# First activation chunk at another place in its 128-byte line, and the residual's transposes moved from the down projection into the up projection

## What is computed

```python
mix_out = jnp.einsum("bsd,de->bse", merged, w_out[layer])
x = x + rms_norm_2(mix_out, mix_norm_post[layer])
h = rms_norm_2(x, ffn_norm_pre[layer])
up = jnp.einsum("bsd,df->bsf", h, w_up[layer])
up = causal_dwconv(up, conv_f_w[layer], conv_f_b[layer])
gate, val = jnp.split(up, 2, axis=-1)
ffn_out = jnp.einsum("bsf,fd->bsd", jax.nn.gelu(gate) * val, w_down[layer])
x = x + rms_norm_2(ffn_out, ffn_norm_post[layer])
```

## Time and profile before

| | us |
|---|---|
| median of 3 runs (lowest, highest) | 1136.49 (1133.57, 1137.23) |
| the profiled execution, its own time | 1134.4 |
| its span, first to last instruction | 1132.6 |
| TensorE busy, of the span | 1109.1 |
| VectorE busy | 786.1 |
| ScalarE busy | 587.8 |
| GpSimd busy | 140.6 |

### The profile page before, as it was taken

How to read it: one execution, slowest core, us unless ns; L and a number is a source line. 1 busy time by engine, 2 the same in 40 slices (tenths; PEclk the granted TensorE clock), 3 DMA queues, 4 the chain that set the end, 5 groups by cost and what they waited for, 6 DMA issues and landing times.

```text
span 1132.6 us, 21593 instructions
## 1 busy us (share of the span) xinstructions
PE 1109.1 (98%) x9351; PEld 1068.6 (94%) x9351; DVE 786.1 (69%) x1134; ACT 587.8 (52%) x828; POOL 140.6 (12%) x109
## 2 busy tenths in 40 slices
PE   7999899999999999999999999999999989999998
PEld 6988799999999999999999997999988989999998
DVE  6567488784457566977644689786475889888752
ACT  4477655443336555544433566854366647666531
POOL 4200050001230005000122206201010000111000
PEclk9999999999999999999999999999999999999999
DMA  9943055566654444555555472666464545556551
GB/s 280 276 150 112 1 184 189 186 195 201 200 187 155 154 139 150 186 187 187 186 187 186 132 212 69 200 200 217 131 221 143 188 147 187 186 187 205 186 184 40
DMA packets 195938, 195.72 MB, mean 173 GB/s; under 512 B 9803, under 2 KB 193028, under 8 KB 195844
## 3 DMA queue, kind: packets, MB, share of 16 engines
q1 hardware_dynamic: 193680, 190.53, 52.9%
q10 hardware_dynamic: 2164, 3.82, 1.1%
HBM read 192.86 MB, written 1.47 MB: 172 GB/s over the span
## 4 chain that ended last, share of the span: by engine, by line
PE 94%; DVE 3%; ACT 2%; DMA 0%; issue 0%; DVEq 0%; SPq 0%; ACTq 0%
PE ps_gemm L1727 50%; PE ps_trans L1727 35%; PE ps_score L1804 2%; PE ps_out L1836 2%; PE ps_trans L1821 2%; DVE act_lo L1144 2%; DVE w_lo L1138 1%; PE ps_gemm L1908 1%; PE ps_score L2035 1%; DMA x_in<-in_x 0%; PE ps_out L2035 0%; PE ps_out L2039 0%; PE ps_score L2039 0%; DVE rs L1150 0%; PE ps_score L1770 0%; ACT prob L798 0%
## 5 line engine op out<-in xcount | busy, mean ns | idle before, releaser
L1138 DVE TENSOR_TENSOR w_lo<-raw,w_hi 128x2048 fp32r<-128x2048 f32 (+2 forms) x179 | 408.2, 2289 | 45.2 <-ACT w_hi L753 45.0
L753 ACT ACTIVATE w_hi<-raw 128x2048 fp32r<-128x2048 f32 (+2 forms) x179 | 332.3, 1863 | 175.2 <-DMA raw<-in_mlp_w 95.3
L1727 PE MATMUL ps_gemm<-act_hi,w_hi 128*128 128x256 f32 (+1 forms) x960 | 267.1, 286 | 4.7 <-ACT act_hi L1064 4.4
L1727 PE MATMUL ps_gemm<-act_hi,w_lo 128*128 128x256 f32 (+1 forms) x960 | 259.9, 282 | 0.0
L1727 PE MATMUL ps_gemm<-act_lo,w_hi 128*128 128x256 f32 (+1 forms) x960 | 254.8, 281 | 0.5 <-DVE act_lo L1144 0.4
L1727 PE MATMUL ps_trans<-act_hi,w_hi 128*128 128x256 f32 x688 | 193.1, 281 | 1.9 <-DVE w_lo L1138 1.9
L1727 PE MATMUL ps_trans<-act_hi,w_lo 128*128 128x256 f32 x688 | 193.0, 281 | 0.0
L1727 PE MATMUL ps_trans<-act_lo,w_hi 128*128 128x256 f32 x688 | 192.9, 280 | 0.0
L1727 PEld LDWEIGHTS ps_gemm<-act_hi,w_hi 128*128 128x128 f32 (+1 forms) x960 | 182.1, 192 | 10.2 <-issue 8.2
L1727 PEld LDWEIGHTS ps_gemm<-act_hi,w_lo 128*128 128x128 f32 (+1 forms) x960 | 178.6, 190 | 0.3
L1727 PEld LDWEIGHTS ps_gemm<-act_lo,w_hi 128*128 128x128 f32 (+1 forms) x960 | 173.7, 186 | 2.1 <-DVE act_lo L1144 0.9
(11 more groups left out here) (379 smaller groups left out, 2238.9 us busy)
## 6 DMA issues: line engine op xcount, KB each, us to landing
raw<-in_mlp_w SPq DMA_DIRECT2D x64, 1024.0 KB, 5.4
raw<-in_w_in SPq DMA_DIRECT2D x30, 1024.0 KB, 5.4
raw<-in_w_up SPq DMA_DIRECT2D x24, 1024.0 KB, 5.2
raw<-in_od_w_in SPq DMA_DIRECT2D x12, 1024.0 KB, 5.1
raw<-in_w_down SPq DMA_DIRECT2D x12, 1024.0 KB, 5.2
raw<-in_ev_w_in SPq DMA_DIRECT2D x9, 1024.0 KB, 8.1
raw<-in_w_proj_a SPq DMA_DIRECT2D x8, 640.0 KB, 4.3
raw<-in_ev_w_out SPq DMA_DIRECT2D x4, 1024.0 KB, 5.1
```

The lines of the kernel that those rows point to most:

```text
L753: act.activation(w_hi[:, slot, 0:k, 0:n], raw[:, slot, 0:k, 0:n], ACT.Copy).then_inc(hi_done, 1)
L1138: dve.tensor_tensor(w_lo[:, slot, 0:k, 0:n], raw[:, slot, 0:k, 0:n], w_hi[:, slot, 0:k, 0:n].bitcast(F32), ALU.subtract).then_inc(w_ready, 1)
L1727: ins = pe.matmul(dst, lhs, rhs, start=(first and opens and opening), stop=(last and closes and i + 1 == len(order)), skip_group_check=True)
```

## The change

Chunk 0 of `act_hi` gets a tensor of its own, 32 bytes past the place that it had; the other seven chunks start 1152 bytes past the old start, 128 more than before, and so keep their place in a 128-byte line. `act_lo` is laid out likewise. Scratch and arena start 256 bytes later. `act_hi` and `act_lo` become lists of chunks, so each use picks its chunk; `gemm` gets a small function for that. The 16 transposes of the residual stand behind slab 3 (the fourth) of `f_up`, no longer behind slab 2 of `f_dn`, with the same two waits. No instruction is added or dropped.

```diff
@@ -67,6 +67,8 @@
 PA = 8
 DN_STEP = 10
 RING = 5
+TURN_AT = 3
+FIRST_SHIFT = (32, 32)
 AHEAD = 3
 REL = 384

@@ -191,9 +193,17 @@
     ssq = place("ffn_sums", [P, TB, 4])
     rs_o = place("ffn_rs", [P, TB])
     fw = place("conv_f", [P, 4, 2 * NH2])
-    act_hi = place("act_hi", [P, NX, T], F32R)
-    act_lo = place("act_lo", [P, NX, T], F32R)
-    tmp0 = top[0]
+    acts = top[0]
+
+    def chunks(name, at, shift):
+
+        first = place(f"{name}_first", [P, T], F32R, at + shift)
+        rest = place(name, [P, NX - 1, T], F32R, at + T * 4 + P)
+        return [first[:, :]] + [rest[:, c, :] for c in range(NX - 1)]
+
+    act_hi = chunks("act_hi", acts, FIRST_SHIFT[0])
+    act_lo = chunks("act_lo", acts + NX * T * 4 + P, FIRST_SHIFT[1])
+    tmp0 = acts + 2 * (NX * T * 4 + P)
     arena = tmp0 + 8 * K
     assert arena + 70 * K <= 229344, arena + 70 * K

@@ -757,7 +767,7 @@
-                    act.activation(act_hi[:, c, :], x[:, c, :], ACT.Copy, scale=gain(n, c)).then_inc(xh, 1)
+                    act.activation(act_hi[c], x[:, c, :], ACT.Copy, scale=gain(n, c)).then_inc(xh, 1)
@@ -807,7 +817,7 @@
-                    dst = dob[:, o - 4, :] if pr["kind"] == "diff" else (mix_hi if p < 2 else act_hi)[:, o, :]
+                    dst = dob[:, o - 4, :] if pr["kind"] == "diff" else mix_hi[:, o, :] if p < 2 else act_hi[o]
@@ -1141,8 +1151,8 @@
-                dve.scalar_tensor_tensor(out=act_lo[:, c, :], in0=x[:, c, :], scalar=gain(n, c),
-                                         in1=act_hi[:, c, :].bitcast(F32), op0=ALU.mult, op1=ALU.subtract).then_inc(xl, 1)
+                dve.scalar_tensor_tensor(out=act_lo[c], in0=x[:, c, :], scalar=gain(n, c),
+                                         in1=act_hi[c].bitcast(F32), op0=ALU.mult, op1=ALU.subtract).then_inc(xl, 1)
@@ -1166,7 +1176,6 @@
-            hi, lo = (mix_hi, mix_lo) if p < 2 else (act_hi, act_lo)
@@ -1237,7 +1246,8 @@
-                    dve.tensor_tensor(lo[:, o, :], ps_o[:, seq % 2, 0:T], hi[:, o, :].bitcast(F32), ALU.subtract)\
+                    hi_o, lo_o = (mix_hi[:, o, :], mix_lo[:, o, :]) if p < 2 else (act_hi[o], act_lo[o])
+                    dve.tensor_tensor(lo_o, ps_o[:, seq % 2, 0:T], hi_o.bitcast(F32), ALU.subtract)\
@@ -1695,6 +1705,10 @@
+
+            def chunk(xx, c):
+                return xx[c] if isinstance(xx, list) else xx[:, c, :]
+
@@ -1715,13 +1729,13 @@
-                    lhs = xx[:, kc0 + k, half * P:(half + 1) * P]
+                    lhs = chunk(xx, kc0 + k)[:, half * P:(half + 1) * P]
-                    rhs = xx[:, kc0 + k, :]
+                    rhs = chunk(xx, kc0 + k)
@@ -2080,6 +2094,14 @@
         for j in range(24):
             gemm(s0 + j, g0 + j, act_hi, act_lo, before_chunk=x_in(6) if j == 0 else None, low_last=j == 0,
                  between=stat_at(6, 2) if j == 1 else None)
+            if j == TURN_AT:
+                pe.wait_ge(x_new, 4)
+                pe.wait_ge(sd_ok, 7)
+                for tb in range(TB):
+                    for c in range(NX):
+                        ins = pe.transpose((ps_s, ps_o)[tb][:, c // 4, c % 4 * P:(c % 4 + 1) * P],
+                                           x[:, c, tb * P:(tb + 1) * P], ident[:, :])
+                ins.then_inc(x_tok, 1)
         s0, g0 = st["f_dn"].s0, st["f_dn"].g0
         for j in range(12):
             def ready(pair, r=j % 3):
@@ -2087,14 +2109,6 @@
-            if j == 2:
-                pe.wait_ge(x_new, 4)
-                pe.wait_ge(sd_ok, 7)
-                for tb in range(TB):
-                    for c in range(NX):
-                        ins = pe.transpose((ps_s, ps_o)[tb][:, c // 4, c % 4 * P:(c % 4 + 1) * P],
-                                           x[:, c, tb * P:(tb + 1) * P], ident[:, :])
-                ins.then_inc(x_tok, 1)

```

More of the change, by code:

```diff
@@ L1063, in _ @@
             for c in (2 * gi, 2 * gi + 1):
-                act.activation(act_hi[:, c, :], x[:, c, :], ACT.Copy, scale=gain(6, c)).then_inc(xh, 1)
+                act.activation(act_hi[c], x[:, c, :], ACT.Copy, scale=gain(6, c)).then_inc(xh, 1)
             if gi == 2:
```

## The result

The changed kernel takes 1144.94 us in the median of six runs (1143.55 to 1147.63), the kernel before 1135.03 us beside it (six runs, 1128.69 to 1137.95): a ratio of 1.0107, 95% interval 1.0067 to 1.0147. It is slower, by about 1%. The profiled execution took 1143.55 us with a span of 1141.8 us, 9.2 us above the span of before.

What follows compares the result with a forecast made beforehand. TensorE's matmul spacing was taken as the bound. From 1134.4 us, 16.8 of fast slabs less 1.3 tipping delay and 0.6 borders, plus 0.1, gave 1119.4; allowing for the before median, 2.1 higher, 1119 to 1122, forecast 1121, range 1117 to 1146.

Steps and rivals of the forecast that it cites:

- What bounds the kernel: TensorE, busy 98% of the span: time is the number of L1727 matmuls times their start-to-start distance, at two paces.
- 0.215 us a slab: Claimed difference for 48 matmuls between the slow pace, 5.655 us, and the fast one, 5.440 us; nothing lies between.
- chunks 1 to 7 stay at 64: Activation layout: only chunk 0 changes its place in a 128-byte line; everything behind moves 256 bytes and keeps its place.
- The direct cost of the borders: Place changes around chunk 0 in 115 slabs, two borders each: 0 to 1.2 us, taken as 0.6.
- The Sum: Total for the whole kernel: borders tip 78 reachable slow slabs to fast, up to 16.8 us gained; fast case chance 0.50.
- a steady against an uneven beat: Reason given for the fast pace winning: the steady pace is absorbing, the slow one is an uneven beat of three.
- The borders tip the pace to slow: Rival: the fast pace doesn't survive chunk 0's border; up to 13.5 us lost, 1143 to 1150, middle 1147; chance 0.20.
- discount for what tips by chance: In the slow rival, an amount without its own figure taken off 1136.5 + 13.5, leaving 1143 to 1150.
- The transposes: 16 transposes moved from f_dn to f_up: about 1.75 us moves along, waits already met, net by itself -0.1 us.
- the two extras: At 946.3 in f_up: the 75 ns w_lo wait vanishes; such breaks led to fast four times in five, 4.9 us if lasting.
- The last sentence of the prediction: Said the forecast is wrong altogether if the two paces depend on something that differs from run to run.

Runs made afterwards that it cites:

- e5: Kernel before with act_lo and everything behind it 128 bytes later, transposes in the down projection: 1148.57 us, ratio 1.0137.
- e15: Kernel before with act_lo and everything behind it 256 bytes later: 1129.34 us, ratio 0.9991.
- e8: Kernel before with act_lo and everything behind it 512 bytes later: 1133.67 us, ratio 1.0009.
- e1: Changed kernel with both chunk 0 shifts set to 0, transposes still in the up projection: 1136.53 us, ratio 1.0053.
- e14: Kernel before with only both chunks 0 moved, 96 bytes off modulo 256, behind chunks 1 to 7; arena 256 bytes later: 1123.84 us, ratio 0.9926.
- e13: Kernel before with only both chunks 0 moved, 64 bytes off modulo 256, behind chunks 1 to 7; arena 256 bytes later: 1123.53 us, ratio 0.9944.
- e6: Kernel before with both chunks 0 moved, 32 bytes off modulo 256, behind chunks 1 to 7; arena 128 bytes later: 1148.61 us, ratio 1.0134.
- e10: Kernel before with only both chunks 0 moved, 32 bytes off modulo 256, behind chunks 1 to 7; arena 256 bytes later: 1145.2 us, ratio 1.0101.
- e16: Kernel before with act_hi and everything behind it 64 bytes later, at the weights' own place modulo 256: 1165.31 us, ratio 1.0303.
- e2: Changed kernel with the transposes back in the down projection, chunk 0 still at byte 96: 1143.73 us, ratio 1.0106.
- e18: e13's layout with the 16 transposes behind slab 3 of f_up, against the kernel before: 1122.99 us, ratio 0.991.
- e9: Kernel before with act_lo 128 bytes later, and scratch and arena 256 bytes later: 1147.18 us, ratio 1.0123.
- e4: Changed kernel's layout with chunk 0 shifted by 64 instead of 32 bytes, transposes in the down projection: 1137.23 us, ratio 1.0073.
- e12: Kernel before with only scratch and arena 128 bytes later, activations untouched: 1131.87 us, ratio 0.9979.
- e3: Changed kernel's layout with all eight chunks at byte 96 of a line, transposes in the down projection: 1139.71 us, ratio 1.009.

## Why the prediction was wrong

**What bounds the kernel: right.** The time is the number of matmuls of one line times their distance, and but for the clock in one slab of r_xa nothing else moved: PE busy without a gap in the three stretches, VectorE at 80 of 95 us.

**0.215 us a slab: right in size, too narrow in kind.** Fast and slow slabs are 5440 and 5653 ns, 0.213 apart. But "Nothing lies between" holds for the old layout alone: others gave 5473, 5480, 5627 and 5650 ns, and above both 5706 (e5, r_v) and 5760.

**"chunks 1 to 7 stay at 64": the premise that failed.** I counted places modulo 128. They count modulo 256: e15 and e8 (256, 512) change nothing, e5 (128) takes the fast pace away. In the changed kernel 14 of 16 chunks are untouched by the shift by 32, but the seven of the high part lie at 192; the seven of the low part and all behind moved by 256 and did keep their place. The e1 run, with no shift (and chunk 0 of the low part at 192 too), shows that this alone makes the streamed stages slow: 5623 to 5650 ns, ratio 1.0053.

**The direct cost of the borders, 0.6 us: too small.** A misplaced chunk 0 costs 33 to 40 ns a slab (e14, e13) even where the pace comes back, for all 115 slabs 3.8 to 4.6 us, an estimate. My upper bound of 1.2 us took one border at 776.07 for the whole fault, though TensorE needs eight or nine matmuls to find back.

**The Sum, "I expect the many small disturbances to end in the fast pace": wrong for this change, though such layouts exist.** This is the step that gave the forecast its sign, and of its 16.8 us nothing came by fast slabs: m_dn stayed at 5653 ns, m_up and f_up went to 5627, and the fast stages went slow. With 32 bytes the disturbances end slow, in e6 and e10 with all else in place. With 64 or 96 bytes they end fast wherever the chunks stream, in all 78 slow slabs that I had listed as reachable but the attention's, and the gain is 0.6 to 0.7%. Either pace can absorb; which one it is hangs on the bytes, and I had no row from which to choose the sign. My argument of a steady against an uneven beat was no evidence: 0.50 was too much for it. (The range, said to leave out 1117.6 by a hair, holds it, as it starts at 1117.)

**The rival "The borders tip the pace to slow" came true in its number**, with 1144.94 in its 1143 to 1150, and its mechanism alone gives as much (e6 1.0134, e10 1.0101). In the changed kernel it isn't alone: the stages that stream these chunks are slow without the shift (e1), so a part of the hit is luck. Its pieces came as listed: the first layer's 32 slabs cost 5.8 us, 13 of the third block 2.5, the last nine, which now inherit, 1.8. The argument against it, that the disturbance is half as large, was worth nothing: 64 bytes are kinder than 32. Its discount for what tips by chance came otherwise: slow slabs that stream these chunks take 5627 ns in the new layout, 0.026 us less each (without the shift 5623 and 5650 in turn).

**The transposes: right that nothing waits, wrong on the two extras.** They cost 1.66 us in f_dn before and 1.67 in f_up after. After:

```profile
954.14 1.04 PE L2102 MATMUL ps_score<-ident,x 128*128 128x128 f32 x8
955.01 1.04 PE L2102 MATMUL ps_out<-ident,x 128*128 128x128 f32 x8
955.80 0.36 PE L1741 MATMUL ps_gemm<-act_hi_first,w_hi 128*128 128x256 f32 x1
956.00 0.28 PE L1741 MATMUL ps_gemm<-act_lo_first,w_hi 128*128 128x256 f32 x1
956.12 0.28 PE L1741 MATMUL ps_gemm<-act_hi_first,w_lo 128*128 128x256 f32 x1
```

The wait for w_lo is gone, but the slab behind takes 5.733 us where it took 5.724, since the first distance behind transposes is 0.20 us anyway. That four of five breaks of this kind lead into the fast pace was read from too few cases: of the 14 kernels other than e16 with the same 16 transposes in f_dn, 3 are fast behind them. The inheriting of the last nine slabs was right.

**What the pages would have made of it.** By the Trainium skill, "SBUF — State Buffer", Specifications, lines are 16 bytes, and by that no shift here would matter; the runs differ (e6 against e13, e5 against e15), and the measurement decides. The same page of the Trainium skill, under "Who interferes with whom", gives PE a second read port for LDWEIGHTS, independent of the one for the streamed operand; in e16 the beat is 120.0 instead of 113.3 ns when both operands lie at 128 and not when one does, so here the two are not independent in time.

**From run to run.** The last sentence of the prediction named this too, and it is so for the old layout: it ran from 1123.97 to 1144.08 us over all comparisons. The traces of e8 and e15, which have its places modulo 256, have stages fast that its own has slow (m_up, m_dn, and in e15 f_up), which fits stretches falling to one pace or the other. Layouts that settle the streamed stages scatter less, some far less (e2 1143.53 to 1143.9, e18 1122.79 to 1123.07, but e9 1145.82 to 1152.51).

## What to carry to other kernels

Where matmuls run back to back with a weight load each, compare the same stretch in several stages and several runs. Look at the granted clock first; where it is the same, two lengths for the same count mean a beat that can fall into more than one pace, and then the places of streamed and loaded operand in SBUF modulo 256 are worth a scan of a few values. A single step in one direction is no test of such an idea: with all else in place 32 bytes lost 1% and 64 or 96 won 0.6 to 0.7%, and the same 64 in the layout of the change lost 0.7% (e4). And when a layout edit shifts one buffer, list where every other one lands, modulo more than the line you have in mind.

## What the runs showed of the hardware

- Distance of matmuls of 256 columns, each with a 128 by 128 load, at the 2.4 GHz level: 113.3 or 117.8 ns with activations at 64 and weights at 128 modulo 256, whichever streams; only 117.8 with both streamed parts at 192 and the weights at 128 (e12); 120.0 with all at 128 (e16).
- The pace persists over borders between tensors of the same place (32 slabs at 5440 ns and 32 at 5653 in the kernel before), and one misplaced chunk in eight can reset it, to slow at 96 (e6, 5655 to 5665) and to fast at 128 and 160 (e13, e14, 5480 and 5473).
- After some 2 us in which TensorE waits for w_lo the granted clock falls to the 1.2 GHz level in some executions (before: 213 ns a matmul, 1.5 us lost in one slab) and stays at 2.4 in others (after).
- Loaded operands have such effects as well: in r_v, where activations are loaded, slabs took 5706 ns with hi and lo at 64 and 192 (e5) and at 96 and 224 (e3), 5520 in e4, 5486 in the changed kernel and 5440 in e1. Lengths of 5440 and some 5653 both occur there with all at 64 (before, e15).
- **Open:** why 256 bytes and why these values; what the transposes decide on (behind the same code the pace was slow eleven times and fast three times); whether it is the place 192 or the step to it that ends the fast pace; why a_dn is fast behind the slow a_up in e1 and e4 but not in e2, e3, e9 and e10; whether moving the weights instead would give a layout without any fault.
